# Splitting x from the plain turned residual, with the norm's scale applied behind the up projection

## What is computed

```python
h = h + concat(o_a, o_b, o_c) @ w_out                  # 1024 -> 1024
h = h + conv_glu_ffn(rmsnorm(h, norm_ffn_g), ffn_up, ffn_conv_w, ffn_conv_b, ffn_down)

def rmsnorm(x, g):
    return x * rsqrt(mean(x * x, axis=-1) + 1e-6) * g  # one factor per token, one per feature

def conv_glu_ffn(hn, w_up, conv_w, conv_b, w_down):
    u = hn @ w_up                                      # 1024 -> 5632
    uc = conv_b + sum(conv_w[j] * shifted(u, 2 - j) for j in range(3))   # causal, width 3, along tokens
    gate, val = split(uc, 2)
    return (silu(gate) * val) @ w_down                 # 2816 -> 1024
```

## Time and profile before

| | us |
|---|---|
| median of 3 runs | 1629.16 |
| lowest and highest run | 1624.2, 1629.26 |
| the profiled execution, its own time | 1624.13 |
| its span | 1622.3 |
| seam: last matmul of w_out to first of the up projection | 277.0 to 283.4 in the span |
| up projection | 283.4 to about 416 |
| PE busy over the span | 96% |
| DVE, ACT busy over the span | 73%, 53% |

### The profile page before, as it was taken

How to read it: one execution, slowest core, us unless ns; L and a number is a source line. 1 busy time by engine, 2 the same in 40 slices (tenths; PEclk the granted TensorE clock), 3 DMA queues, 4 the chain that set the end, 5 groups by cost and what they waited for, 6 DMA issues and landing times.

```text
span 1622.3 us, 31723 instructions
## 1 busy us (share of the span) xinstructions
PE 1557.2 (96%) x10650; PEld 1419.6 (88%) x10650; DVE 1182.0 (73%) x2262; ACT 861.5 (53%) x1587; POOL 343.3 (21%) x257
## 2 busy tenths in 40 slices
PE   8899998999999998999999999999999999999997
PEld 8789987999887895898998999988888999999996
DVE  3788676788757568556489678779998777777776
ACT  5664445656557544565555455554444544445444
POOL 3333322011000511222057755530000000000000
PEclk9999999999999989999999999999999999999999
DMA  8333245555663620254546644467777665656654
GB/s 279 118 109 100 92 143 158 174 163 180 188 195 117 244 78 1 79 182 143 169 153 198 204 144 146 135 191 243 242 241 226 198 187 183 192 183 190 183 187 149
DMA packets 87849, 271.16 MB, mean 167 GB/s; under 512 B 9824, under 2 KB 26336, under 8 KB 87392
## 3 DMA queue, kind: packets, MB, share of 16 engines
q1 hardware_dynamic: 65088, 237.01, 46.5%
q10 hardware_dynamic: 22688, 33.16, 6.3%
HBM read 258.60 MB, written 11.53 MB: 167 GB/s over the span
## 4 chain that ended last, share of the span: by engine, by line
PE 78%; DVE 12%; ACT 4%; issue 2%; POOL 1%; DMA 1%; ACTq 0%; DVEq 0%; SPq 0%; POOLq 0%
PE ps_chunk L488 42%; PE ps_misc L488 21%; PE ps_misc L295 7%; PE ps_misc L2468 4%; PE ps_chunk L295 2%; DVE ffn_arena L1584 1%; ACT w_hi L421 1%; PE ps_misc L798 1%; DVE w_lo L428 1%; POOL w_lo L428 1%; DVE mixers_arena L2265 1%; DVE mixers_arena L2268 1%; DVE mixers_arena L2269 1%; PE ps_chunk L495 1%; DVE mixers_arena L2264 1%
## 5 line engine op out<-in xcount | busy, mean ns | idle before, releaser
L421 ACT ACTIVATE w_hi<-raw 128x512 fp32r<-128x512 f32 (+1 forms) x900 | 548.7, 626 | 493.5 <-PE ps_chunk L488 285.9
L428 DVE TENSOR_TENSOR w_lo<-raw,w_hi 128x512 fp32r<-128x512 f32 x671 | 489.7, 745 | 275.1 <-ACT w_hi L421 265.5
L488 PE MATMUL ps_chunk<-x_hi,w_hi 128*128 128x256 f32 x1792 | 518.3, 289 | 14.8 <-POOL w_lo L428 7.6
L488 PE MATMUL ps_chunk<-x_hi,w_lo 128*128 128x256 f32 x1792 | 508.0, 283 | 0.0
L488 PE MATMUL ps_chunk<-x_lo,w_hi 128*128 128x256 f32 x1792 | 507.9, 283 | 0.0
L428 POOL TENSOR_TENSOR w_lo<-raw,w_hi 128x512 fp32r<-128x512 f32 (+2 forms) x229 | 300.5, 1327 | 546.4 <-ACT w_hi L421 483.1
L488 PEld LDWEIGHTS ps_chunk<-x_hi,w_hi 128*128 128x128 f32 x1792 | 344.2, 192 | 27.4 <-POOL w_lo L428 12.9
L488 PEld LDWEIGHTS ps_chunk<-x_hi,w_lo 128*128 128x128 f32 x1792 | 344.4, 192 | 2.8 <-issue 0.2
L488 PEld LDWEIGHTS ps_chunk<-x_lo,w_hi 128*128 128x128 f32 x1792 | 344.2, 192 | 0.0
L488 PE MATMUL ps_misc<-w_hi,hid_hi 128*128 128x512 f32 x520 | 203.4, 391 | 2.1 <-DVE hid_lo L2547 1.4
L488 PE MATMUL ps_misc<-w_hi,hid_lo 128*128 128x512 f32 x520 | 203.1, 391 | 0.0
(11 more groups left out here) (342 smaller groups left out, 1746.9 us busy)
## 6 DMA issues: line engine op xcount, KB each, us to landing
raw<-in_stream SPq DMA_DIRECT2D x452, 512.0 KB, 3.6
early_rows<-row ACTq DMA_DIRECT2D x64, 128.0 KB, 1.7
row<-early_rows ACTq DMA_DIRECT2D x62, 128.0 KB, 3.2
memory_kv<-mixers_arena ACTq DMA_DIRECT2D x4, 512.0 KB, 5.0
mixers_arena<-in_cmp_w ACTq DMA_DIRECT2D x1, 2048.0 KB, 9.5
mixers_arena<-memory_kv ACTq DMA_DIRECT2D x4, 512.0 KB, 6.3
mixers_arena<-in_consts ACTq DMA_DIRECT2D x1, 1729.0 KB, 8.1
row<-in_rows ACTq DMA_DIRECT2D x3, 512.0 KB, 6.9
```

What stands on the lines that cost most here:

```text
L421: e.activation(w_hi[q % 2][:, s], raw[q][:, s], ACT.Copy).then_inc(made, 1)
L428: e.tensor_tensor(w_lo[q % 2][:, s], raw[q][:, s], w_hi[q % 2][:, s].bitcast(F32), ALU.subtract).then_inc(made, 1)
L488: last = e.matmul(o, stationary[a], moving[b], start=start and i == 0, stop=stop and i == 2, skip_group_check=True)
```

## The change

The root of the norm is no longer needed for x. `h` is turned by the identity, and split with the feature gain alone. `HalfOfX` does that for four of the eight feature tiles: the first half's turning stands in the last unit of w_out, the second's directly behind the add. The inverse root is made beside the first chunk of the up projection: ACT sums the squares of both tokens' tiles (`own_square`) and takes the root (`own_root`), DVE inverts it and spreads it into a 128x256 tile (`own_inverse`), PE turns this behind the first chunk (`turn_scales`), and DVE keeps the result (`keep_scales`) in `per_token`, a 128x256 tile with each token's factor in every partition.

In the first hook DVE now waits for `s_use`, multiplies the chunk's 128x1024 result by `per_token` into a new SBUF buffer `US` (one instruction), and releases `ps_chunk` at once (`s_ev`). ACT's newest tap waits for that instruction (`s_scaled_u`) and reads `US`; so do DVE's eight older taps.

The squares of the first half, the dozen matmuls on the identity and the 16 multiplications by diagonals are gone. The order of the streams of weights, and everything after the feed-forward network, stays.

```diff
@@ woven_projection
+                    if last and (part, some) == turn_at and gain is not None:
+                        ends_of[name] = [(lane.sem, lane.n) for lane in work]
+                        half = HalfOfX(h, 0, gain)
+                        half.turn((s_ev, first + 1), (s_ev, first + 1))
+                        half.highs()
@@ ffn
-            t = normed_x(lambda k: c("norm_ffn_g", k), added)
-            first, count = multiply("ffn_up", False, t)
+            US = cut(2, 4 * T)
+            x_halves = [half_of["w_out"], HalfOfX(h, 4, lambda k: c("norm_ffn_g", k))]
+            x_halves[1].turn(*added)
+            second_high, second_low = second_unit()
+            second_high()
+            x_halves[1].highs()
+            second_low()
+            for x_half in x_halves:
+                x_half.lows()
+            def own_square(t):
+                return lambda e: e.activation(xn[:, t, :], h[:, t, :], ACT.Square,
+                                              accum_out=ss[:, 2 + t:3 + t]).then_inc(s_own_square, 1)
+            def own_inverse(e):
+                e.wait_ge(s_own_root, 1)
+                e.reciprocal(inverse, over_root).then_inc(s_wide, 1)
+                e.wait_ge(s_wide, 1)
+                e.tensor_copy(wide, inverse.unsqueeze(2).broadcast_to([P, TT, P])).then_inc(s_wide, 1)
+            def turn_scales(e):
...
+                for t in range(TT):
+                    last = e.transpose(ps[:, t * P:(t + 1) * P], wide[:, t, :], ident)
+                last.then_inc(s_turned, 1)
+            def keep_scales(e):
+                e.wait_ge(s_turned, 1)
+                e.tensor_copy(per_token, ps[:, 0:T]).then_inc(s_scales, 1)
+            first, count = multiply("ffn_up", False, BothHalves(*x_halves), after_first=turn_scales)
@@ newest_tap
-                e.wait_ge(s_use, m * UNITS + UNITS)
+                e.wait_ge(s_scaled_u, i + 1)
...
-                    last = e.activation(UC[:, slot, piece, :], ps_chunk[slot][:, piece * T:(piece + 1) * T],
+                    last = e.activation(UC[:, slot, piece, :], US[:, slot, piece * T:(piece + 1) * T],
@@ older_taps
+                e.wait_ge(s_use, m * UNITS + UNITS)
+                if isinstance(i, int) and i == 0:
+                    e.wait_ge(s_scales, 1)
+                e.tensor_tensor(US[:, slot, :].rearrange("p (k t) -> p k t", t=T),
+                                ps_chunk[slot][:, :].rearrange("p (k t) -> p k t", t=T),
+                                per_token.unsqueeze(1).broadcast_to([P, 4, T]), ALU.mult).then_inc(s_scaled_u, 1)
+                e.wait_ge(s_scaled_u, i + 1)
+                e.sem_inc(s_ev, 1)
...
-                        e.scalar_tensor_tensor(out=o, in0=ps_chunk[slot][:, piece * T:(piece + 1) * T - lag],
+                        e.scalar_tensor_tensor(out=o, in0=US[:, slot, piece * T:(piece + 1) * T - lag],
...
-                e.wait_ge(s_sum, i * 8 + 8)
-                e.sem_inc(s_ev, 1)
@@ split_chunks of ffn
+            act.quiet(own_square(0), *added)
+            split_chunks(first, count, act_hooks=(newest_tap, gate_silu), dve_hooks=(older_taps, gated), more=down_count,
+                         act_lead={2: own_square(1), 3: own_root}, dve_lead={3: own_inverse, UNITS: keep_scales})
```

More of the change, by code:

```diff
@@ L230, in build @@
         picks = sb("picks", [P, 3, T])
-        ss = sb("ss", [P, 20])
+        ss = sb("ss", [P, 40])
         ident, iota = ident_iota[:, 0:P], ident_iota[:, P:2 * P]
@@ L445, in hook, with after @@
                             hooks[part](e, slot, n - 1)
+                    def after(u):
+                        if isinstance(n, int) and n == first and u in lead:
+                            lead[u](e)
                     for q in range(begin, 2):
@@ L577, in body @@
                         last.then_inc(used_up, 1)
+                if after_first and isinstance(n, int) and n == first:
+                    after_first(e)
             over_chunks(pe, first, count, body)
@@ L646, in woven_first_two, with woven_first_halves, high, run @@
             pe.quiet(high if i < 4 else low)
-        def dense(first, count, token_major, evac, *needs, by_k=(), pairs=1, func=lambda n: ACT.Copy):
+        def woven_first_halves(u, ps, left, by_k, i):
+            units = [(ps[:, q * T:(q + 1) * T], (w_hi[q], w_lo[q])) for q in range(2)]
+            def high(which, tiles):
+                def run(e):
+                    if which[0] == 0 and tiles[0] == 0 and u:
+                        e.wait_ge(*left)
+                    for k in tiles:
+                        e.wait_ge(*by_k[k][0])
+                        for q in which:
+                            o, w = units[q]
+                            if k % 4 == 0:
+                                e.wait_ge(halves_of_unit[k // 4][1], u + q + 1)
+                            high_x(e, o, w, k, k == 0 and q == 0)
+                return run
+            def low(q, part):
+                def run(e):
+                    o, w = units[q]
+                    low_x(e, o, w, range(4 * part, 4 * part + 4), by_k).then_inc(halves_of_unit[part][2], 1)
+                return run
+            pe.quiet((high((0,), (0, 1, 2, 3)), high((1,), (0, 1, 2, 3)), high((0, 1), (4, 5)), high((0, 1), (6, 7)),
+                      low(0, 0), low(0, 1), low(1, 0), low(1, 1))[i])
+        def dense(first, count, token_major, evac, *needs, by_k=(), pairs=1, func=lambda n: ACT.Copy, midway=None,
+                  scale=None):
             def left_by(n):
@@ L679, in dense @@
                 for i in range(8):
-                    woven_first_two(units[0], ps_chunk[first % pairs], left_by(first)[0], by_k, i)
+                    if midway and i == 1:
+                        midway()
+                    (woven_first_halves if midway else woven_first_two)(
+                        units[0], ps_chunk[first % pairs], left_by(first)[0], by_k, i)
                     if i == 4:
@@ new lines, in build, with __init__, __getitem__, squares_of_tile @@
+        class BothHalves:
+            def __init__(self, *halves):
+                self.halves = list(halves)
+            def __getitem__(self, k):
+                half = self.halves[k // 4]
+                return half.high[k], half.low[k]
+        def squares_of_tile(t, at, *needs, scratch=None):
+            return act.do(lambda e: e.activation(xn[:, t, :] if scratch is None else scratch, h[:, t, :], ACT.Square,
+                                                 accum_out=ss[:, at + t:at + t + 1]), *needs, own=False)
@@ L907, in add_projection, with woven_projection @@
             return [(s_sum, sums + t + 1) for t in range(TT)]
-        def woven_projection(name, order, x_parts, needs):
+        def woven_projection(name, order, x_parts, needs, gain=None, turn_at=(0, 0)):
             first, _ = STREAM[name]
@@ L916, in woven_projection @@
             parts, sums = parts_made[0], sums_made[0]
-            parts_made[0], sums_made[0] = parts + TT, sums + TT
+            parts_made[0], sums_made[0] = parts + (TT if gain is None else 0), sums + TT
             def first_half(e):
@@ L936, in second_half @@
                                     ALU.add).then_inc(s_sum, 1)
+                    if gain is not None and t == 0:
+                        split_lo(e, 0, first + 2, (1,))
                 e.wait_ge(s_sum, sums + TT)
@@ L1535, in build @@
               memory=(0, 2, memory_tokens()))
-        ends = [lane.now() for lane in work] + [(s_kv[0], 32), (s_kv[1], 32)]
+        assert after_turn["w_out"] == [lane.n for lane in work]
+        ends = ends_of["w_out"] + [(s_kv[0], 32), (s_kv[1], 32)]
         for lane in work:
             lane.wait(*ends)
-        dve.wait((s_lo1, dense_end[0]))
         plain = lambda k: c("one")
```

85 lines of the change are left out of this document (72 added, 13 removed).

## The result

| | before | after |
|---|---|---|
| median (lowest to highest), 4 runs each | 1629.21 (1624.2 to 1633.51) | 1656.28 (1651.99 to 1664.24) |
| ratio of the times, 95% interval | | 1.0156 [1.0117, 1.0195] |
| the profiled execution, its own time | 1624.13 | 1651.99 |
| its span | 1622.3 | 1650.2 |

The account below looks back on a forecast made before the run. It took PE, level with the taps' chain in each up-projection chunk, to bound the kernel. 1624.1 + 23.3 (hooks) - 2.3 (seam) + 9 (clock) = 1654.1, plus 2 towards the median: 1656 us, range 1641 to 1669.

Parts of the forecast that it names:

- The bound: Up projection: PE and the taps' chain are level, so time put into that chain comes out as PE idle, once per chunk.
- The steady hook: First hook in the up projection's loop: the multiplication delays the taps, net 2.1 us for each of 8 chunks, 16.8 us.
- A: Start of PE's next instruction after a chunk's end in the up projection, 331.63 in the earlier trace; hook times count from it.
- The second hook: Up projection, written-out body of the second first-hook: 1.9 us lost, with hardly any register instructions; the same for the eleventh.
- Nothing for taps from SBUF: Taps of the up projection: reading SBUF instead of PSUM saves nothing, 473 to 484 ns against 468 to 485.
- Rival (c): Up projection's taps: cheaper from SBUF, each 0.05 us off the 88 taps giving 4.4 us; 1640 to 1648, chance 0.07.
- The seam: Between w_out and the up projection: PE resumes with unit 2 earlier, a gain of 2.3 us, ends 0 and 3.9.
- the load of `p`: At the seam: issued behind four `x_hi` near 281.3, landing at 284.0, so PE resumes with unit 2 at 287.4.
- rival (e): At the seam: the load of `p` eats the whole gain, 2.3 us more; no chance of its own given.
- The clock: PE's twelve longer waits, seam and up projection: granted clock falls behind one in two, 1.5 us each, 9 us.
- rival (a): PE's longer waits: the clock doesn't fall, 21 us lost, 1645 by the profile, up to 1650 by the median; chance 0.23.
- The sum: Whole kernel: 1654.1 us on the profile's scale, plus 2 us towards the median, 1656 us; chance of the forecast case 0.58.

## Why the prediction was right, and where only its sum was

**The bound: right.** The earlier trace rows said that the taps' chain and PE were level within 0.3 us, and that anything put into it would show at unit 2. The hooks alone bring the loss, their removal takes it away to the hundredth (132.17 us), and their place behind unit 2 too.

**The steady hook: right in every step.** Against A: the multiplication was to start at A+1.40 and started at A+1.28; ACT's tap 2.85, came 2.82; the first older tap 4.02, came 4.09; PE 5.99 + 2.1 = 8.09, came 8.16. The loop's chunks grew by 2.05 to 2.15 us, where 2.1 stood. The second hook took 1.93 (1.9), the first 2.41 (2.75; which part of it was too dear I didn't trace). All eleven: 23.1 measured, 23.3 predicted. Not every microsecond put into the chain came out, though: the unread multiplication of 1.22 us cost 0.66, as it covered waits. What I had not said is how the hook divides: two thirds of the hook are the way over ACT, which the unread multiplication showed.

**Nothing for taps from SBUF: right.** One line's durations, as in the earlier trace rows (ns minimum, median, maximum):

```profile
L1758 DVE SCALAR_TENSOR_TENSOR ffn_arena<-ffn_arena,col x88: 473/478/486, 294.7 to 441.5; 128x255 f32<-128x255 f32 x44, 128x254 f32<-128x254 f32 x44
...
L1732 ACT ACTIVATE ffn_arena<-ffn_arena,col x44: 586/588/603, 293.6 to 438.9; 128x256 f32<-128x256 f32 x44
```

The taps take 478 ns from SBUF and took 474 from PSUM. Rival (c) did not happen, and the advice of the Trainium skill ("VectorE: DVE Perf Modes", "Rules for kernel authors") to copy to SBUF first has nothing to give for this instruction of three operands. ACT's tap became dearer, 588 ns for 559.

**The seam: right in sign, low in size.** 3.6 us of gain instead of 2.3, and the wait of 1.9 us ahead of unit 2 is one of 0.16. The step that failed is the place of the load of `p`: I had it issued behind four `x_hi` of 0.45 us each. It goes out at 278.15 in the trace, 0.23 us behind the start of the first of them and before the other three have started (278.29 to 279.49). In the kernel before, too, it went out at 284.76, while ACT's last two `x_hi` ran (284.36 to 285.23), which I had read as behind them. On the forecast's scale, with the 1.66 us added, it went out at 279.8 where I had 281.3. ACT still waits 1.41 us for `p`, and the squares stand behind it, but PE could resume at 286.2 instead of 287.4; and PE itself was done with units 0 and 1 at 286.0 instead of 285.5. Between the two, 0.16 us are left of the wait. So rival (e) was wrong as well.

**The clock: the term that was mis-sized.** I gave twelve waits one chance in two, and 1.5 us each: 9 us. The price was right, 1.5 us. The number was not: the clock fell behind two of eleven waits in this trace, three of eleven in the hooks alone, two of eleven in the kernel with `ss` of 36 floats. Two and two from four gaps were too few to say one half. The term is 3.0 us in this trace and 3 to 4.5 in the three. On this term rival (a), with none, was nearer than the 9 us of the forecast. Nor do the falls look like independent draws, as I had taken them: in each of the three traces the low stretches lie four waits, 58.0 us, apart (they begin at 342.3 and 400.3; at 305.6, 363.7 and 421.7; at 327.9 and 385.9). Why just these waits is open.

**The sum: right by terms that cancel.** On the scale of the profile I had 1654.1 and 1651.99 was measured. The clock was 6 us too high, the hooks 0.2, the seam's gain 1.3 too low, and three things that I had not counted make up for most of it: the down projection's 1.7 us by placement, 2.0 us to the end (partly a stretch of low clock that begins at 919), and 3.4 less 1.7 us in the second block's mixers and ahead of the seam, which go with where the clock happened to fall outside the change's reach. For the 3.4, windows of the second block's mixers; of before:

```profile
584.00:588.00 4.00, 4.00 (x20) 3.89 (x21) 0.00 (x0) 0.96 (x3) 0.00 (x0) 0.50 0.02 6
...
604.00:608.00 4.00, 4.00 (x32) 2.96 (x24) 3.73 (x14) 1.50 (x4) 0.00 (x0) 0.61 0.00 0
...
652.00:656.00 4.00, 3.95 (x25) 3.55 (x23) 3.90 (x5) 2.69 (x6) 0.00 (x0) 0.64 0.00 0
```

and of after, 22.6 to 25.9 us later, where the same work runs:

```profile
608.00:612.00 4.00, 4.00 (x23) 3.89 (x23) 0.00 (x0) 1.68 (x4) 0.67 (x1) 0.57 0.00 0
...
624.00:628.00 4.00, 4.00 (x36) 2.41 (x35) 3.76 (x14) 0.74 (x3) 0.00 (x0) 0.50 0.00 0
...
648.00:652.00 4.00, 4.00 (x34) 2.03 (x36) 3.21 (x6) 0.59 (x3) 0.39 (x1) 0.50 0.00 0
...
676.00:680.00 4.00, 3.19 (x14) 2.79 (x15) 3.70 (x9) 3.49 (x11) 0.00 (x0) 0.60 0.00 0
```

Four places for three, and 23.9 us at the low clock for 20.5. The kernels differ in that stretch of the table above by up to 6.6 us (206.8 before, 210.2 after, 213.4 with the taps behind unit 2, where the low clock lasted 30.7 us) though none of them touches that code. The 2 us that I added for the way from a profiled execution to the median were 4.3, which closed the rest. So 1656 for 1656.28 is partly luck; the mechanism and the 23 us of hooks are not.

**What stays open:** which addresses make the 128x512 matmuls slower; the 1 us behind the second block's memory attention in the kernels built on the change; and which waits of 2 us the clock falls behind, of which the runs show only that they are the minority, four waits apart.

## What to carry to other kernels

When an engine's wait is short but comes once in each turn of a loop, two chains are level, and the next thing put into the shorter-looking one is paid for, with its hand-overs to other engines and less only the waits that it covers in that chain, whatever the busy shares say. Before giving such work up, look for the instruction that the late engine really waits for and put it ahead of the work: the eleven multiplications cost 23 us with the taps ahead of unit 2's split and nothing with the taps behind it. Price a dependence between two engines apart from the instruction itself (here 0.7 us for the instruction and 1.4 for the way over ACT).

## What the runs showed of the hardware

- The same stream of 128x512 matmuls, without waits and at a granted clock of 1.00, ran at one per 0.227 us or one per 0.233 us by where tiles lie in SBUF, after 80 bytes of shift (64 bytes gave 0.233 too). It is 1.7 us in a stretch of 59.
- ACT's activation of 128x256 with scale and bias took 588 ns from SBUF and 559 from PSUM; DVE's multiply-add of 128x255 took 478 ns from SBUF and 474 from PSUM.
- A matmul of 128x128 in fp32 on the identity stands in the trace as two instructions of 0.12 us each: 14 made 28 and 3.29 us, 8 made 16 and 1.95 us.
- Behind waits of 2.0 to 2.4 us the granted clock fell to 0.50 in two, three and two of eleven cases (three kernels), at 1.5 us each, four waits apart. Behind ten waits of each of two kernels that PE was kept busy in, for 1.95 us or for the whole of the wait, and behind waits of 0.8 to 1.2 us in the kernel with the unread multiplication, it never fell.
